# Two pieces of each later modulation vector on TensorE's column tiles, six on VectorE, and the row joined by GpSimd

## The chip, the cores and the metric

The kernel runs on one core of a Trainium2 chip. What counts is the device time of one execution in microseconds (us), as a median of several. Times of single instructions come from one profiled execution, in microseconds from the start of its span unless marked ns. TensorE (PE) has a queue of its own for weight loads (PEld); VectorE is DVE, ScalarE is ACT, GpSimd is POOL, SyncE is SP. A name with a q behind it (SPq, ACTq) is an engine's issuing of DMAs.

## What is computed

Two transformer-like blocks over 1024 tokens of width 1024, everything in float32. The first block is what matters here:

```python
mod = (jax.nn.silu(c) @ ada_w[l] + ada_b[l]).reshape(bsz, 6, dm)
shift_a, scale_a, gate_a = mod[:, 0, None, :], mod[:, 1, None, :], mod[:, 2, None, :]
shift_f, scale_f, gate_f = mod[:, 3, None, :], mod[:, 4, None, :], mod[:, 5, None, :]
h = rms_norm(x, norm1_g[l]) * (1.0 + scale_a) + shift_a
proj = h @ w_in[l]
y_m = mlstm_group(...)      # recurrence over chunks, with gates from proj
y_p = pool_group(...)       # window means of part of proj, then a product
mix = jnp.concatenate([y_m, y_p], axis=-1) @ w_out[l]
x = x + gate_a * mix        # then a mixture of experts over rms_norm(x)
```

The second block (attention and a feed-forward layer) has a modulation of its own, `silu(c_2) @ w_ada_2 + b_ada_2`. So there are twelve modulation vectors of 1024, each the product of one row of 1024 with a 1024x1024 matrix of 4 MB. Two of them (shift_a, scale_a) are needed at once; the other ten are the "later" vectors.

## The kernel before

The program is a row of phases (`mixer`, `moe`, `attention`, `fox_out_mlp`), with a barrier of all engines behind each of the first. The change lies in `mixer`, lines 131 to 1270.

**The projections.** `proj = h @ w_in` is cut into NT = 17 tiles of 128 columns (`tiles`): u0 to u3, the gates g, o0 to o3, p0 to p3, v0 to v3. Product n is tile n times all 1024 tokens, in two halves of 512, each 8 x 3 matmuls (every float32 factor is split into a high and a low float32r part, `split_mm`, lines 1762 to 1768): 48 matmuls. Tile n of w_in is loaded (`weights`), copied to its high part by ScalarE (`high(n)`, line 536) and its low part is taken by VectorE (`low(n)`, line 761, the tile `w_in_low`). VectorE's iteration n ("slot n") ends with `low(n + 2)`; TensorE waits for it (s_lo) ahead of product n + 2. ScalarE evacuates each half product (`evac`) and turns the products of tiles p into silus of u along the way.

**The later vectors.** The matrix of a vector is cut into eight pieces of 128x1024 floats (512 KB): row 8p + k of the matrix is partition p of piece k. Seven pieces (DK = 7) are summed by VectorE (`piece(j)`, line 757): acc = piece * csil[:, k] + acc, where the bias, or zero on the other partitions, is the first addend. acc holds two vectors in turns. The eighth piece is multiplied on TensorE with csil's last column as a one-column stationary operand (line 1132), and the column of ones sums acc over the partitions onto it (line 1135). The two halves of the row go to bank 6, partition 0, and bank 7, partition 32, two column tiles of the array. ScalarE copies the row from PSUM (`mod_row(b)`, lines 577 and 578) and issues its store to `modulation_rows`.

**The order.** `quota` says how many pieces VectorE sums in each slot, `until` its running sum, and `summed_in[b]` the product behind which TensorE sums vector b: now 2, 3, 5, 6, 8, 9, 10, 11, 12, 13. `mod_row(b)` stands in ScalarE's iteration summed_in[b] + 1, ahead of that iteration's evacuations. SyncE loads the pieces in order into three slots of the tile `v_aug` (`spare`), each when VectorE has used the piece three before; the last piece of a vector goes to a fourth slot, from the same queue (`last_piece`, line 300). A slot has other work too: convolutions of u in slots 1 to 4, the gate rows (`gate_rows`, a chain of recurrences over four partitions) in slot 6 behind low(8), window sums of p in slots 11 to 14. ScalarE's iterations 5 and 7 have Exp and Ln for the gate rows.

**Behind the vectors.** SyncE loads w_out's row blocks over acc, the bias tile and x_square (`out_weights`), GpSimd multiplies them with the gate row (`gated_weights`, line 472), then builds the first decay matrix (`decay_log`, line 455), and the loop over eight chunks of tokens starts.

## Time and profile before

| | us |
|---|---|
| median of 3 executions | 2497.85 |
| all three | 2503.66, 2495.33, 2497.85 |
| the profiled execution | 2499.09 |
| its span | 2497.5 |
| TensorE busy | 2400.2 (96%) |
| VectorE busy | 1915.3 (77%) |
| ScalarE busy | 1354.0 (54%) |
| GpSimd busy | 590.3 (24%) |

A row of the profile names line, engine, operation, output and inputs; behind "x" stands how many instructions it merges. In a timeline the first number is the start, the second the time from the first start to the last end; in brackets stands how long the engine was idle ahead of it and what ended this. Matmuls are pipelined, so that 0.39 us of one matmul overlap with the next; how far apart they start tells their pace. A float32 matmul leaves two records.

### The profile page before, as it was taken

What the parts mean: (1) busy time and instruction counts of PE and PEld (TensorE: products, weight loads), DVE (VectorE), ACT (ScalarE), POOL (GpSimd) and SP (SyncE); (2) the same over time, 40 slices, a digit from 0 to 9 for tenths busy, and PEclk for the clock granted to TensorE, in tenths of its full rate; (3) what the DMA queues carried; (4) which work ended last, traced back from release to release, by engine and by line L of the source; (5) the groups of instructions that cost most, each with busy time, mean ns of one, the idle gap of its engine ahead of it and who ended that gap; (6) DMA issues with size and microseconds to landing.
All of it is one profiled execution on the core that took longest, in us unless ns stands there. A gap on an engine that the chain in (4) does not pass through costs nothing. (4 is left out here: it accounts for less than half of the span.)

```text
span 2497.5 us, 33891 instructions
## 1 busy us (share of the span) xinstructions
PE 2400.2 (96%) x11969; PEld 1979.8 (79%) x11969; DVE 1915.3 (77%) x2471; ACT 1354.0 (54%) x1924; POOL 590.3 (24%) x492
## 2 busy tenths in 40 slices
PE   7999999899999999999989999999999999999999
PEld 4766678678888887886688999997788888878887
DVE  4876668678989989897877888887766666657786
ACT  3243323357777777775676676776434444444332
POOL 2000444143333233332711111110042333400000
PEclk8999999999999999999999999999999999999999
DMA  6778255589878899998521111113332443587864
GB/s 253 237 246 297 102 208 206 227 318 397 336 270 308 307 398 395 411 394 337 193 69 51 52 52 51 52 39 116 129 110 86 152 167 139 188 314 260 304 252 152
DMA packets 181316, 535.36 MB, mean 214 GB/s; under 512 B 17711, under 2 KB 77715, under 8 KB 167881
## 3 DMA queue, kind: packets, MB, share of 16 engines
q1 hardware_dynamic: 147260, 462.82, 50.6%
q0 software_dynamic: 12592, 45.63, 4.8%
q10 hardware_dynamic: 21340, 25.29, 2.9%
q8 instruction: 75, 1.23, 0.2%
q14 instruction: 49, 0.39, 0.1%
HBM read 443.38 MB, written 90.33 MB: 214 GB/s over the span
## 5 line engine op out<-in xcount | busy, mean ns | idle before, releaser
L1766 PE MATMUL psum<-w_high,block_hT_high 128*128 128x512 f32 x576 | 232.5, 404 | 6.9 <-DVE w_low L1384 5.7
L1384 DVE TENSOR_TENSOR w_low<-first_w_up,w_high 128x2048 fp32r<-128x2048 f32 x72 | 186.5, 2628 | 53.1 <-ACT w_high L1378 53.1
L1768 PE MATMUL psum<-w_high,block_hT_low 128*128 128x512 f32 x576 | 225.3, 391 | 0.0
L1767 PE MATMUL psum<-w_low,block_hT_high 128*128 128x512 f32 x576 | 224.8, 390 | 0.0
L1766 PE MATMUL psum<-w_qkv_high,fox_hT_high 128*128 128x384 f32 (+1 forms) x512 | 181.6, 355 | 8.5 <-DVE w_qkv_low L2613 3.4
L1384 DVE TENSOR_TENSOR w_low<-first_w_gate,w_high 128x2048 fp32r<-128x2048 f32 x74 | 168.6, 2282 | 19.6 <-ACT w_high L1378 19.4
L1766 PE MATMUL psum<-w_mlp_out_high,hidden_part_high 128*128 128x512 f32 x448 | 174.5, 390 | 3.3 <-DVE hidden L4011 1.8
L1480 POOL TENSOR_TENSOR block_out<-block_out,late_rows 128x1024 f32<-128x1024 f32 x35 | 92.7, 2648 | 359.6 <-ACT block_out L1644 359.6
L1378 ACT ACTIVATE w_high<-first_w_gate 128x2048 fp32r<-128x2048 f32 x74 | 141.2, 1912 | 65.4 <-DMA first_w_gate<-in_w_expert_gate 61.6
L1767 PE MATMUL psum<-w_mlp_out_low,hidden_part_high 128*128 128x512 f32 x448 | 174.3, 389 | 0.0
L1768 PE MATMUL psum<-w_mlp_out_high,hidden_part_low 128*128 128x512 f32 x448 | 174.3, 389 | 0.0
L1768 PE MATMUL psum<-w_qkv_high,fox_hT_low 128*128 128x384 f32 (+1 forms) x512 | 173.7, 339 | 0.0
L1767 PE MATMUL psum<-w_qkv_low,fox_hT_high 128*128 128x384 f32 (+1 forms) x512 | 173.7, 339 | 0.0
L1766 PE MATMUL psum<-mix_hT_high,w_in_high 128*128 128x512 f32 x400 | 163.0, 408 | 3.6 <-DVE w_in_low L761 2.1
L1384 DVE TENSOR_TENSOR w_low<-first_w_down,w_high 128x2048 fp32r<-128x2048 f32 x70 | 156.8, 2277 | 2.4 <-ACT w_high L1378 2.4
L1767 PE MATMUL psum<-mix_hT_low,w_in_high 128*128 128x512 f32 x400 | 157.6, 394 | 0.0
L3763 ACT ACTIVATE hidden_part_high<-hidden_part 128x1024 fp32r<-128x1024 f32 x54 | 57.2, 1060 | 175.8 <-PE psum L1768 171.6
L1766 PEld LDWEIGHTS psum<-w_high,block_hT_high 128*128 128x128 f32 x576 | 108.4, 188 | 42.2 <-DVE w_low L1384 19.2
L1378 ACT ACTIVATE w_high<-first_w_down 128x2048 fp32r<-128x2048 f32 x70 | 130.5, 1915 | 19.5 <-DMA first_w_down<-in_w_expert_down 12.8
L1378 ACT ACTIVATE w_high<-first_w_up 128x2048 fp32r<-128x2048 f32 x72 | 133.9, 1915 | 0.6 <-DMA first_w_up<-in_w_expert_up 0.6
L1768 PEld LDWEIGHTS psum<-w_high,block_hT_low 128*128 128x128 f32 x576 | 108.1, 188 | 23.9
L1767 PEld LDWEIGHTS psum<-w_low,block_hT_high 128*128 128x128 f32 x576 | 108.3, 188 | 20.9 <-issue 0.2
(524 smaller groups left out, 6732.3 us busy)
## 6 DMA issues: line engine op xcount, KB each, us to landing
first_w_gate<-in_w_expert_gate SPq DMA_DIRECT2D x32, 2048.0 KB, 10.0
first_w_up<-in_w_expert_up SPq DMA_DIRECT2D x32, 2048.0 KB, 10.4
first_w_down<-in_w_expert_down SPq DMA_DIRECT2D x31, 2048.0 KB, 10.5
w_mlp_out_quarters<-in_w_mlp_out SPq DMA_DIRECT2D x78, 512.0 KB, 7.0
hidden_part<-hidden_parts SPq DMA_DIRECT2D x54, 512.0 KB, 4.4
v_aug<-in_w_ada SPq DMA_DIRECT2D x48, 512.0 KB, 5.1
expert_rows<-block_out POOLq DMA_DIRECT2D x34, 512.0 KB, 8.3
v_aug<-in_ada_w SPq DMA_DIRECT2D x32, 512.0 KB, 4.8
```

The lines of the kernel that those rows point to most:

```text
L1378: act.activation(wh[:, par, half], raw[kind][:, half], ACT.Copy).then_inc(s_wh, 1)
L1384: dve.tensor_tensor(wl[:, par, half], raw[kind][:, half], wh[:, par, half].bitcast(F32), ALU.subtract).then_inc(s_wl, 1)
L1480: pool.tensor_tensor(ob[:, u, :], ob[:, u, :], grow, ALU.mult).then_inc(s_om, 1)
L1766: pe.matmul(out, sh, mh, start=start, stop=False)
L1767: pe.matmul(out, sh, ml, start=False, stop=False)
L1768: return pe.matmul(out, sl, mh, start=False, stop=stop)
L3763: act.activation(sph[u][:, ij], h_split(gc, ij), ACT.Copy).then_inc(q_sh, 1)
```

## The change

Of a later vector's eight pieces VectorE now sums six (DK = 6). The seventh is loaded into the second half of the bias tile, the eighth into the fourth slot, both by ScalarE's queue (`last_pieces`, called at the start of the `mod_row` of the vector before). TensorE multiplies the seventh onto partitions 64 (bank 6) and 96 (bank 7) and the eighth, with the sums of acc, onto 0 and 32 as before. ScalarE copies both rows, one into acc's own first partition; GpSimd adds them (`join_row`) and issues the store. A vector's first piece on VectorE waits for the join of the vector two before, where it waited for its sums; the biases share one row. The quotas are cut anew: slots 0 to 8 had 7, 4, 3, 4, 3, 7, 6, 6, 6 pieces and have 7, 4, 3, 3, 3, 6, 6, 2, 6. `summed_in` becomes 2, 3, 5, 6, 7, 9, 10, 11, 12, 13. The loads of w_out all wait for the last row's store.

```diff
...
         later = [(0, q) for q in range(2, 6)] + [(1, q) for q in range(6)]
-        DK = KT - 1
+        DK = KT - 2
         NP = DK * len(later)
-        quota = [7, 4, 3, 4, 3, 7] + [6] * (NT - 6)
+        quota = [7, 4, 3, 3, 3, 6, 6, 2] + [6] * (NT - 8)
         until = [min(NP, sum(quota[:n + 1])) for n in range(NT)]
...
 
-        def sums_row(hf):
-            return bank[6 + hf][32 * hf:32 * hf + 1, :]
+        def sums_row(hf, at=0):
+            return bank[6 + hf][at + 32 * hf:at + 32 * hf + 1, :]
 
...
 
-                def last_piece(b):
-                    l, q = later[b]
-                    if b == 0:
-                        sp.wait_ge(s_gain, 1)
-                    else:
-                        sp.wait_ge(s_ms, b)
-                    sp.dma_start(spare[:, 3, :], ada[l][:, DK, q * D:(q + 1) * D]).then_inc(s_ml, 16)
-
                 def piece(j):
...
                     if k == 0:
-                        if b < 2:
+                        if b == 0:
                             sp.wait_ge(s_f0, 1)
                         else:
-                            sp.wait_ge(s_ma, DK * (b - 2) + 1)
-                        sp.dma_start(bt[0:1, b % 2, :], ada_bias[l][:, q * D:(q + 1) * D]).then_inc(s_mb[b % 2], 16)
+                            sp.wait_ge(s_ma, DK * (b - 1) + 1)
+                        sp.dma_start(bt[0:1, 0, :], ada_bias[l][:, q * D:(q + 1) * D]).then_inc(s_mb[0], 16)
                     if j >= 3:
...
                         piece(sent)
-                        if sent % DK == 2 and sent > DK:
-                            last_piece(sent // DK - 1)
                         sent += 1
-                    if n + 1 < NT and until[n + 1] == NP and until[n] < NP:
-                        last_piece(len(later) - 1)
 
...
                 sp.wait_ge(s_ms, len(later))
-                for n in range(4):
+                sp.wait_ge(s_mw, 16 * len(later))
+                for n in range(5):
                     out_weights(n)
-                sp.wait_ge(s_mw, 16 * len(later))
-                out_weights(4)
                 sp.dma_start(shift2, mods[SHIFT_F:SHIFT_F + 1, :].to_broadcast([P, D])).then_inc(d_rows, 16)
...
                     pool.tensor_tensor(stat[:, t, 1:2], stat[:, t, 0:1], mhalf[:], ALU.pow).then_inc(s_rs, 1)
+                def join_row(b):
+                    l, q = later[b]
+                    pool.wait_ge(s_me, b + 1)
+                    pool.tensor_tensor(mrow, mrow, acc[0:1, b % 2, :], ALU.add).then_inc(s_mx, 1)
+                    pool.wait_ge(s_mx, b + 1)
+                    pool.dma_start(mods[6 * l + q:6 * l + q + 1, :], mrow).then_inc(s_mw, 16)
+
+                join_row(0)
+                join_row(1)
                 pool.wait_ge(cv, 4 * HM)
...
                 pool.memset(rr[:, 3, 0:S:P], 0.0).then_inc(r_z, 1)
+                for b in range(2, len(later)):
+                    join_row(b)
 
...
 
+                def last_pieces(b):
+                    l, q = later[b]
+                    if b == 0:
+                        act.wait_ge(s_gain, 1)
+                    act.dma_start(bt[:, 1, :], ada[l][:, DK, q * D:(q + 1) * D]).then_inc(s_ml, 16)
+                    act.dma_start(spare[:, 3, :], ada[l][:, DK + 1, q * D:(q + 1) * D]).then_inc(s_ml, 16)
+
                 def mod_row(b):
-                    l, q = later[b]
                     act.wait_ge(s_ms, b + 1)
+                    if b + 1 < len(later):
+                        last_pieces(b + 1)
                     if b >= 1:
                         act.wait_ge(s_mw, 16 * b)
+                    act.activation(acc[0:1, b % 2, 0:HALF], sums_row(0, 64), ACT.Copy)
+                    act.activation(acc[0:1, b % 2, HALF:D], sums_row(1, 64), ACT.Copy)
                     act.activation(mrow[:, 0:HALF], sums_row(0), ACT.Copy)
                     act.activation(mrow[:, HALF:D], sums_row(1), ACT.Copy).then_inc(s_me, 1)
-                    act.wait_ge(s_me, b + 1)
-                    act.dma_start(mods[6 * l + q:6 * l + q + 1, :], mrow).then_inc(s_mw, 16)
 
...
                 weights(2)
+                last_pieces(0)
                 act.wait_ge(par, 16 * 8)
...
                     if k == 0:
-                        dve.wait_ge(s_mb[b % 2], 16 * (b // 2 + 2))
+                        dve.wait_ge(s_mb[0], 16 * (b + 2))
                         if b >= 2:
-                            dve.wait_ge(s_ms, b - 1)
-                        added = bt[:, b % 2, :]
+                            dve.wait_ge(s_mx, b - 1)
+                        added = bt[:, 0, :]
                     else:
...
                         if summed_in[b] == n:
-                            pe.wait_ge(s_ml, 16 * b + 16)
+                            pe.wait_ge(s_ml, 32 * b + 32)
                             if b >= 1:
...
                             for hf in range(2):
-                                pe.matmul(sums_row(hf), csil[:, l, DK:KT], spare[:, 3, hf * HALF:(hf + 1) * HALF], start=True, stop=False)
+                                pe.matmul(sums_row(hf, 64), csil[:, l, DK:DK + 1], bt[:, 1, hf * HALF:(hf + 1) * HALF], start=True, stop=True)
+                            for hf in range(2):
+                                pe.matmul(sums_row(hf), csil[:, l, DK + 1:KT], spare[:, 3, hf * HALF:(hf + 1) * HALF], start=True, stop=False)
                             pe.wait_ge(s_ma, DK * (b + 1))
```

## Rows read from the trace of the kernel before

**Rows 1.** The page: the chain that ended last, share of the span by engine.

```profile
PE 27%; DVE 1%; DMA 1%; issue 0%; ACT 0%; SPq 0%; DVEq 0%; ACTq 0%
```

**Rows 2.** Busy time of each engine by stage: stretch, length, busy (count), clock, DMA share, GB/s.

```profile
84.50:169.00 84.50, 82.61 (x370) 62.47 (x369) 69.05 (x57) 30.51 (x40) 1.05 (x2) 1.00 0.71 225
169.00:253.40 84.40, 75.74 (x313) 51.22 (x311) 58.03 (x53) 28.72 (x40) 0.00 (x0) 0.94 0.84 281
253.40:297.40 44.00, 41.88 (x179) 31.74 (x178) 24.16 (x26) 10.80 (x16) 19.00 (x9) 1.00 0.28 102
```

**Rows 3.** Timeline of TensorE: start, length, what, idle time ahead and releaser.

```profile
95.36 1.03 PE L1132 MATMUL psum<-v_aug,c_silu 128*1 128x512 f32 x4
96.21 1.03 PE L1135 MATMUL psum<-mod_acc,ones 128*1 128x512 f32 x4
...
175.57 1.87 PE L1132 MATMUL psum<-v_aug,c_silu 128*1 128x512 f32 x4 [2.81 <-DMA v_aug<-in_w_ada]
177.23 1.61 PE L1135 MATMUL psum<-mod_acc,ones 128*1 128x512 f32 x4
180.95 0.50 PE L1766 MATMUL psum<-mix_hT_high,w_in_high 128*128 128x512 f32 x1 [2.11 <-DVE w_in_low L761]
...
193.64 1.03 PE L1132 MATMUL psum<-v_aug,c_silu 128*1 128x512 f32 x4
...
223.06 1.87 PE L1132 MATMUL psum<-v_aug,c_silu 128*1 128x512 f32 x4 [2.66 <-DMA v_aug<-in_w_ada]
...
251.60 1.03 PE L1132 MATMUL psum<-v_aug,c_silu 128*1 128x512 f32 x4
...
264.47 1.88 PE L1069 MATMUL psum<-yT,wpool 128*128 128x512 f32 x4
```

**Rows 4.** Groups by line: busy us, mean ns, idle time before them and its releasers.

```profile
L1132 PE MATMUL psum<-v_aug,c_silu 128*1 128x512 f32 x40 | 12.0, 680 | 7.8 <-DMA v_aug<-in_w_ada 6.5 <-DMA v_aug<-in_ada_w 1.2
```

**Rows 5.** Timeline of VectorE, slots 6 and 7.

```profile
152.28 4.06 DVE L757 SCALAR_TENSOR_TENSOR mod_acc<-v_aug,c_silu,mod_acc 128x1024 f32<-128x1024 f32 x3 [4.23 <-DMA v_aug<-in_w_ada]
156.26 1.22 DVE L761 TENSOR_TENSOR w_in_low<-w_in_tile,w_in_high 128x1024 fp32r<-128x1024 f32 x1
...
169.24 1.28 DVE L757 SCALAR_TENSOR_TENSOR mod_acc<-v_aug,c_silu,mod_acc 128x1024 f32<-128x1024 f32 x1
...
179.67 1.22 DVE L761 TENSOR_TENSOR w_in_low<-w_in_tile,w_in_high 128x1024 fp32r<-128x1024 f32 x1
```

**Rows 6.** Timeline of ScalarE and its queue.

```profile
140.99 0.57 ACT L577 ACTIVATE x_square<-psum 1x512 f32<-1x512 f32 x1
...
180.92 0.57 ACTq L545 DMA_DIRECT2D w_in_tile<-in_w_in  x1
181.54 0.60 ACT L566 ACTIVATE sigmoid_oT<-psum 128x512 f32<-128x512 f32 x1 [6.04 <-DVE w_in_low L761]
...
209.62 1.14 ACT L549 ACTIVATE ucT<-ucT,param_cols 128x1024 f32<-128x1024 f32 x1
```

**Rows 7.** Timeline of GpSimd behind the vectors.

```profile
261.69 4.72 POOL L472 TENSOR_TENSOR mod_acc<-mod_acc,w_in_tile 128x1024 f32<-128x1024 f32 x2 [7.97 <-DMA mod_acc<-in_w_out]
...
273.04 3.45 POOL L472 TENSOR_TENSOR x_square<-x_square,w_in_tile 128x1024 f32<-128x1024 f32 x1
284.98 1.04 POOL L455 TENSOR_TENSOR yT<-gate_rows,packed_cols 128x512 f32<-128x512 f32 x1 [8.49 <-issue]
```

**Rows 8.** DMA issues: count, KB each, median us from issue to landing.

```profile
v_aug<-in_w_ada SPq DMA_DIRECT2D x48, 512.0 KB, 5.1
w_in_tile<-in_w_out SPq DMA_DIRECT2D x1, 512.0 KB, 3.4
```

**Rows 9.** Window sums 3 on VectorE beside GpSimd, and TensorE behind them.

```profile
267.48 3.36 DVE L824 TENSOR_TENSOR yT<-yT 128x1023 f32<-128x1023 f32 x1
...
277.75 1.21 DVE L824 TENSOR_TENSOR yT<-yT 128x1016 f32<-128x1016 f32 x1
...
282.02 1.53 PE L1069 MATMUL psum<-yT,wpool 128*128 128x512 f32 x3 [2.12 <-ACT yT L584]
```

More of the change, by code:

```diff
@@ L195, in mixer @@
         s_mp = [sem(f"m_piece{n}") for n in range(3)]
-        s_ma, s_ms, s_me, s_mw, s_ml = [sem("m_" + n) for n in ("acc", "sums", "row", "stored", "last_piece")]
+        s_ma, s_ms, s_me, s_mw, s_ml, s_mx = [sem("m_" + n) for n in ("acc", "sums", "row", "stored", "last_pieces", "row_joined")]
         s_x = [sem(f"y_x{n}") for n in range(4)]
```

## Prediction

> **What bounds the kernel now.** I read the page first, then busy time by stage, then TensorE in order of time, and only then the engines that TensorE waits for. The page [rows 1] is to show that the chain which ended last lies in later phases. The kernel is a row of phases with a barrier behind each, so what the mixer wins or loses reaches the end one for one unless a later wait of the mixer eats it. The stages [rows 2] show the stretch that the change touches: from 84.50 (product 2 begins; product n is the 48 matmuls of w_in tile n) to 253.42 (product 14 begins). TensorE is idle little in the first half (82.61 busy of 84.50), and for 8.7 us of the second, where its granted clock also falls (0.94 on average: mostly 2.4 GHz, 1.2 GHz for short stretches). Behind 253.40 the DMA share is only 0.28: the modulation vectors are over.
>
> In order of time [rows 3] product 14 begins at 251.60 + 1.82 = 253.42. Twelve products at 48 x 0.2267 = 10.9 us (matmul records come 0.227 us apart) are 131 us, ten groups of sums at 1.8 us (95.36 to 97.17) are 18, three groups of transposes 2.6: 151.5 of 168.9 us. **The whole prize is 17.4 us.** Of it 7.8 is TensorE waiting for a vector's last piece [rows 4], 2.11 is a wait for w_in_low of tile 9, 0.6 another wait, and most of the rest is the low clock behind such waits: the eight sum matmuls at 175.57 take 3.3 us for 1.8, those at 223.06 as long, and product 9, from 180.95 to 193.64, takes 12.7 for 10.9.
>
> Why they are late: one SyncE queue loads seven of eight pieces into three slots and must wait for VectorE to free a slot before it can issue anything behind, the last piece too. VectorE [rows 5] takes 1.35 us a piece (4.06 for three) and 1.2 for a w_in_low, and stands still for the ten steps of the gate rows from 157.4 to 169.24; the pieces left over then push w_in_low 9 to 179.67.
>
> **Part 1: VectorE takes six pieces, TensorE two.** Removed: ten VectorE pieces, 13.4 us, none of it on the path by itself. Added: two M=1 matmuls a vector in column tiles 64 and 96. Now two calls in tiles 0 and 32 start together: four L1132 records take 0.85 us (95.36 to 96.21), where four records of a 128-column fp32 product, L1069, take 1.72 [rows 3]. All four tiles side by side cost nothing; in pairs, 0.85 x 10 = 8.5 us, less where TensorE waits anyway. I take 0 to 1, since the second passes and the next loads start as soon as their own tile is free, and keep 8.5 for the range.
> The Trainium skill (TensorEngine Tiling (Array Packing), Key Properties) says that different tiles load weights and multiply in parallel, and gives 128x32 mode four tiles: by it the term is 0. The trace shows it for two tiles only; no row of before has four.
>
> **Part 2: the last two pieces go to ScalarE's queue.** They no longer stand behind slot waits. The waits of 7.8 us go, and with them the low clock of the 223.06 group (1.5). The price: each DMA issue holds ScalarE for about 0.5 us (ACTq 0.57 at 180.92, next activation at 181.54, [rows 6]). I take 0.9 for two pieces of plain rows, ahead of the copies of the row. With two more copies, mod_row grows from 1.2 to 0.9 + 4 x 0.59 = 3.3 us. Evacuation of a product's first half is due 5.4 us into it, so this hides; what is queued behind it matters below.
>
> **Part 3: GpSimd joins.** No row has its add on 1 partition. Nearest is 128x1024, 4.72 us for two [rows 7]; bounds 1.0 (the 128x512 adds) and 3.4 (the slowest 128x1024 one, beside VectorE); I take 2.4, since ScalarE's copy of 1x512 takes what its 128x512 takes (0.57 and 0.60, [rows 6]): one partition is no cheaper. The store is 0.6 us of issue, and its landing must lie between 1 and 8.3 us (a 512 KB store from that queue). The next mod_row stands 7 us later, so ScalarE does not wait for it in the middle of the range. Two joins stand ahead of GpSimd's memsets for the gate rows, which VectorE needs only at 157.4; the first two vectors are summed behind products 2 and 3, some 45 us earlier.
>
> **Part 4: the new wait.** VectorE may start vector b only when the row of b-2 is joined (s_mx). Before, it waited for the sums alone. Behind this wait stand four pieces and the w_in_low of tile n+2, and behind that TensorE. Let T be the end of product n that carries vector b-2's sums. Sums are done at T+1.9; ScalarE by then has an evacuation, a w_in_high and, in tiles p, a silu (1.14, [rows 6]), and starts mod_row at T+2.65, done T+5.9; the join is done at T+8.4. VectorE does three pieces from full slots (4.0 us). The fourth is asked for when the first is used, T+9.7, and lands 4.8 to 5.1 later ([rows 8]: median 5.1): used by T+15.9, w_in_low at T+17.1. TensorE wants it at T + 1.9 + 10.9 + 1.8 = T+14.6. This circle (sums, row, join, pieces, w_in_low, product) matters: **wherever a vector starts in each slot, TensorE can be held to (10.9 + 17.1)/2 = 14.0 us a slot**, about the pace of before (product 10 at 193.64 + 1.8 + 0.85 = 196.3, product 14 at 253.42: 14.3 for each of four), against 12.8 if TensorE ruled.
>
> **The chain, in profile time.**
> Until product 6 (136.5) I change nothing: the wait in slot 2 is about 3 us and the slack before w_in_low 6 takes it.
> Slot 5: vector 4 starts here now. Its wait, for row 2, meets ScalarE in Exp and Ln with their table loads until 140.99 [rows 6]. 140.99 + 3.3 + 2.4 = 146.7; two pieces and w_in_low 7 end at 150.6. Product 7 began at 150.71, so the 1.2 us of the wait removed at product 6's end comes back as this one.
> Slot 6: six pieces, the last three bound by landing (5 us behind use of the slot): w_in_low 8 at 163.5, before 157.4; product 8 at 163.7, before 161.7.
> Gate rows: 11.9 us to 175.4. Then two pieces where there were six with landing waits (169.24 to 179.67), w_in_low 9 at 179.3: product 9 at **179.3 against 180.95**, behind an idle stretch of near 5 us, so with the low clock again (+1.7, between the 1.5 and 1.8 of before).
> Product 9 ends at 192.0, product 10 starts at 194.7 (196.3 before). Silu needs a table load here (1.28): row 5 is joined at 201.8 and w_in_low 11 is out at 210.5, where TensorE is ready at 207.6. Product 11 at 210.5, with the low clock; product 12 at 225.0; product 13 waits for row 7 (223.2 + 17.1): 240.3; product 14 at 253.2 to 254.9.
> Before: 253.42. So over the stage **0 to +1.5 us, I take +0.5**: 10 to 12 us of waits removed, as much put in.
>
> **Part 5: the tail.** W_out loads now all wait for the last store. Before, the first was in use at 261.69, 8.3 us behind product 14's start [rows 7]. Now they are asked for at product 13's end + 1.9 + 2.4 + 2.4 + 0.6 + 2 to 4, or 8 to 10 us behind product 14's start, and the first lands 5 us later. GpSimd's five gatings (15 us) start near +14 instead of +8.3 and end at +29, still ahead of their successor decay_log (284.98, +31.5), so nothing there. But window_sums 3 starts at +14 and then lies wholly beside them: one add took 3.36 us for 1.21 beside GpSimd [rows 9], and TensorE already waits 2.12 us for that block's end at 282.02. One more such collision is 2.15; none is 0. I take +0.7.
> The Trainium skill (SBUF — State Buffer, section Who interferes with whom) says that a VectorE op with two SBUF inputs and a GpSimd op that reads SBUF exclude each other for a whole instruction. The trace agrees (3.36 against 1.21). By the page each of ten joins may cost the sum such a wait. What the rows give is one wait of 2.15 us a meeting, and in the slots that decide VectorE stands idle for the join, so there is nothing to meet.
>
> **Sum:** +0.5 + 0.7 = +1.2 on an execution of 2499.09 us (span 2497.5 and 1.6 around it), which was 1.2 above the median. From the median 2497.85 that is **2499 us**.
>
> **Rivals.**
> 1. *The circle is shorter, faster.* If the join takes 1.0 us, issues cost ScalarE little and the fourth piece lands in 3.4 (the one w_out load that is alone on its queue, [rows 8]), the circle shrinks by 1.4 + 0.7 + 1.5 = 3.6: T+13.5, under TensorE's T+14.6. Then product 9 starts at 177.5 and product 14 at 177.5 + 1.7 + 13.65 + 4 x 12.8 = 244 to 246: 7.5 to 9.5 less, **2489 to 2491**. Against it: one partition was no cheaper on ScalarE, and the DMA is busy 0.84 of 169 to 253. 0.27 for the case, 0.22 that it passes 0.3%.
> 2. *Landing under load, slower.* ScalarE's 1 MB and a w_in tile are asked for just as VectorE's fourth piece is. A piece at 152.28 was waited for 4.23 us [rows 5]; my circle has 2.1. If 4.2 is the rule, w_in_low 8, 11 and 13 come 2.1 us later each and the delays add up, since 11 hangs on product 9 and 13 on 11: 1.2 + 6.3 + 1.7 for one more low clock = +9.2, **2507**, 2506 to 2508. It decides from a wait of about 4 us on. 0.17.
> 3. *The four tiles run in pairs.* +0.85 where TensorE rules (some six vectors): +5, **2503**, still within. 0.12.
> The forecast's case has 0.44. Faster by over 0.3% (7.5 us, about what a measurement can tell) 0.22, slower 0.19 (rival 2's 0.17 and 0.02 for pairs with late landings), the same 0.59. The range of 8 in 10 goes from 2488 (rival 1 nearly whole) to 2508.
>
> **What would show it.** Right: L1132 no longer waits for DMA; VectorE's idle time shows the join at the first piece of vectors 4, 6, 7 and 8; TensorE waits for w_in_low before products 9, 11 and 13; product 14 begins between 252 and 256. Part 1: eight records of the new and old first sums within 0.9 us, or 1.7. Part 3: the join 2.4 us. Wrong if w_in_low comes in time throughout: then product 14 begins before 247; or if product 9 begins behind 182.

## The result: slower, by 0.46%

| | before | after |
|---|---|---|
| median, us | 2497.66 (12 executions) | 2509.43 (12 executions) |
| lowest to highest | 2492.85 to 2504.61 | 2502.80 to 2516.67 |
| profiled execution / its span | 2499.09 / 2497.5 | 2508.58 / 2507.0 |

The ratio is 1.0046, 95% interval 1.0033 to 1.0059. The forecast was 2499, or +1.2 us and no change to be measured, with a range up to 2508. The measured +11.8 us has the small sign that was forecast, but it is ten times the size, clear of the noise and above the range.

I cut the mixer into three parts. "Stage" runs from the first sums (the end of product 2) to the start of product 14; "tail" from there to the first matmul of the loop over chunks; the rest is the span behind that.

| | first sums at | product 14 at | stage | loop at | tail | rest |
|---|---|---|---|---|---|---|
| before | 95.36 | 253.42 | 158.06 | 299.83 | 46.41 | 2197.7 |
| after | 93.15 | 257.75 | 164.60 | 309.87 | 52.12 | 2197.1 |

Stage **+6.5** (forecast +0.5), tail **+5.7** (forecast +0.7), start-up -2.2, rest -0.5: together the 9.5 us between the spans. The first sums come anywhere between 91.9 and 95.7 in the profiles of this study, so the start-up's part is no effect of the change.

The chain that ended last, by engine, on the page of after (answers [rows 1]):

```profile
PE 28%; DVE 1%; issue 0%; ACT 0%; DVEq 0%
```

As in [rows 1], it says only that the end of the program is TensorE's. The stages of after (stretch, length, busy and count of PE, PEld, DVE, ACT, POOL, then clock, DMA share, GB/s; answer [rows 2]):

```profile
84.50:169.00 84.50, 80.85 (x380) 59.54 (x379) 62.12 (x50) 34.13 (x47) 13.72 (x10) 1.00 0.75 243
169.00:253.40 84.40, 72.02 (x311) 52.43 (x310) 53.03 (x47) 33.32 (x48) 14.55 (x9) 0.94 0.77 254
253.40:297.40 44.00, 39.05 (x160) 27.97 (x159) 31.67 (x29) 11.37 (x17) 22.75 (x12) 0.92 0.28 106
```

TensorE is idle 12.4 us in the second stretch where it was 8.7, at the same mean clock (0.94). VectorE does less in the first two (115.2 us against 127.1), and TensorE still waits for it. The waits of the two engines between 84 and 260, groups by line (answer [rows 4]; busy us, mean ns, idle time ahead and its releasers):

```profile
L1775 PE MATMUL psum<-mix_hT_high,w_in_high 128*128 128x512 f32 x193 | 78.5, 407 | 13.9 <-DVE w_in_low L768 13.9
L1139 PE MATMUL psum<-mod_bias,c_silu 128*1 128x512 f32 x40 | 10.3, 590 | 1.4 <-DMA v_aug<-in_w_ada 1.4
...
L764 DVE SCALAR_TENSOR_TENSOR mod_acc<-v_aug,c_silu,mod_acc 128x1024 f32<-128x1024 f32 x45 | 59.7, 1326 | 20.2 <-DMA v_aug<-in_w_ada 14.8 <-DMA v_aug<-in_ada_w 3.2
L764 DVE SCALAR_TENSOR_TENSOR mod_acc<-v_aug,c_silu,mod_bias 128x1024 f32<-128x1024 f32 x8 | 10.3, 1285 | 32.9 <-POOL x_square L435 32.4 <-DMA v_aug<-in_w_ada 0.5
```

The wait of [rows 4] went from 7.8 to 1.4, as forecast. In its place TensorE waits 13.9 us for w_in_low, and VectorE stands 32.4 us for GpSimd's join at the first pieces of vectors (before: 35.8 us for pieces in flight, none for a row).

Here is one slot in full, from w_in_low 10 to w_in_low 11 (start, length, what; idle time ahead and its releaser). VectorE and GpSimd:

```profile
193.91 1.22 DVE L768 TENSOR_TENSOR w_in_low<-w_in_tile,w_in_high 128x1024 fp32r<-128x1024 f32 x1
...
202.28 2.38 POOL L435 TENSOR_TENSOR x_square<-x_square,mod_acc 1x1024 f32<-1x1024 f32 x1 [16.22 <-ACT x_square L586]
...
204.79 1.28 DVE L764 SCALAR_TENSOR_TENSOR mod_acc<-v_aug,c_silu,mod_bias 128x1024 f32<-128x1024 f32 x1 [6.24 <-POOL x_square L435]
206.18 2.67 DVE L764 SCALAR_TENSOR_TENSOR mod_acc<-v_aug,c_silu,mod_acc 128x1024 f32<-128x1024 f32 x2
209.84 1.28 DVE L764 SCALAR_TENSOR_TENSOR mod_acc<-v_aug,c_silu,mod_acc 128x1024 f32<-128x1024 f32 x1 [0.98 <-DMA v_aug<-in_w_ada]
211.04 1.22 DVE L768 TENSOR_TENSOR w_in_low<-w_in_tile,w_in_high 128x1024 fp32r<-128x1024 f32 x1
```

and ScalarE with its queue in the same slot:

```profile
195.16 0.55 ACTq L543 DMA_DIRECT2D w_in_tile<-in_w_in  x1
195.75 0.60 ACT L562 ACTIVATE yT<-psum 128x512 f32<-128x512 f32 x1 [8.93 <-DVE w_in_low L768]
195.86 0.55 ACTq L574 DMA_DIRECT2D mod_bias<-in_w_ada  x1
196.25 1.05 ACT L534 ACTIVATE w_in_high<-w_in_tile 128x1024 fp32r<-128x1024 f32 x1
196.45 0.92 ACTq L575 DMA_DIRECT2D v_aug<-in_w_ada  x1
197.31 1.28 ACT L547 ACT_TABLE_LOAD   x1
198.61 1.15 ACT L547 ACTIVATE ucT<-ucT,param_cols 128x1024 f32<-128x1024 f32 x1
199.79 0.59 ACT L583 ACTIVATE mod_acc<-psum 1x512 f32<-1x512 f32 x1
...
201.60 0.59 ACT L586 ACTIVATE x_square<-psum 1x512 f32<-1x512 f32 x1
...
212.29 0.55 ACTq L543 DMA_DIRECT2D w_in_tile<-in_w_in  x1
```

Read it as a ring. ScalarE stands 8.93 us behind VectorE's w_in_low 10, because it issues the load of the w_in tile three ahead (L543), whose buffer w_in_low frees. Only then come its evacuation, w_in_high, a silu with its table load, and the four copies of the row; then the join; then VectorE's four pieces and w_in_low 11, which ends at 212.26, and ScalarE issues the next such load at 212.29. **The ring holds no product of TensorE.** It takes 17.1 us here, 16.5 and 16.0 in the next two slots, where sums and a product need 12.8. Within these three rings VectorE also waits for pieces in flight, for 0.98, 1.88 and 1.10 us; the rest is work and hand-overs. TensorE's starts of products 9, 10, 11, 13 and 14 follow it (answers [rows 3]; product 12 starts at 228.80):

```profile
178.83 0.67 PE L1775 MATMUL psum<-mix_hT_high,w_in_high 128*128 128x512 f32 x1 [4.39 <-DVE w_in_low L768]
...
195.18 0.50 PE L1775 MATMUL psum<-mix_hT_high,w_in_high 128*128 128x512 f32 x1 [0.71 <-DVE w_in_low L768]
...
212.31 0.50 PE L1775 MATMUL psum<-mix_hT_high,w_in_high 128*128 128x512 f32 x1 [3.51 <-DVE w_in_low L768]
...
244.81 0.50 PE L1775 MATMUL psum<-mix_hT_high,w_in_high 128*128 128x512 f32 x1 [1.39 <-DVE w_in_low L768]
...
257.75 0.50 PE L1775 MATMUL psum<-mix_hT_high,w_in_high 128*128 128x512 f32 x1
```

In the tail (answers [rows 7, 9]; VectorE's last w_in_low and its window sums 3 beside GpSimd's gatings, TensorE behind them):

```profile
269.19 5.70 POOL L470 TENSOR_TENSOR mod_acc<-mod_acc,w_in_tile 128x1024 f32<-128x1024 f32 x2 [4.59 <-DMA mod_acc<-in_w_out]
...
270.58 2.05 DVE L768 TENSOR_TENSOR w_in_low<-w_in_tile,w_in_high 128x1024 fp32r<-128x1024 f32 x1 [4.36 <-ACT w_in_high L534]
...
272.62 3.34 DVE L831 TENSOR_TENSOR yT<-yT 128x1023 f32<-128x1023 f32 x1
276.00 2.22 DVE L830 COPY yT<-yT 128x2 f32<-128x2 f32 x1
...
282.78 2.23 DVE L830 COPY yT<-yT 128x8 f32<-128x8 f32 x1
...
289.18 3.75 PE L1076 MATMUL psum<-yT,wpool 128*128 128x512 f32 x4 [4.95 <-ACT yT L590]
292.72 1.92 PE L1065 MATMUL psum<-ident,yT 128*128 128x128 f32 x8
```

and in the kernel before the same w_in_low, and the last small copy, free of GpSimd:

```profile
266.25 1.25 DVE L761 TENSOR_TENSOR w_in_low<-w_in_tile,w_in_high 128x1024 fp32r<-128x1024 f32 x1 [5.03 <-ACT w_in_high L536]
...
277.68 0.17 DVE L823 COPY yT<-yT 128x8 f32<-128x8 f32 x1
```

The w_in_low begins 12.83 us behind product 14's start in both kernels. In after it takes 2.05 us where it took 1.25, and the block meets GpSimd four times (3.34, 2.22, 2.25, 2.23) where it met it three times (3.36, 2.23, 2.25). That makes 2.8 us: TensorE resumes at 31.43 behind product 14's start, 28.60 before. It waited 4.95 us where it waited 2.12, and now the clock is low behind it: 3.54 us from the first of these four matmuls to the next group, which took 1.79 before, 1.57 for the next eight (0.79), and 0.35 more for the half product. That is the other 2.9 us of the tail's 5.7. I read these by starts, since records overlap: at full clock a matmul's record lasts 0.39 us and the next starts 0.23 behind it. The granted clock from 289.1 to 294.3 is 0.50 (1.2 GHz); before it was 1.00 from 282.0 to 284.6.

The length of the wait alone does not decide this clock. From these four matmuls to the half product behind them the kernel before takes 2.58 us, at full clock, behind its wait of 2.12; y3 and z2 take as long behind waits of 2.83 and 2.84. But x3 takes 1.7 us more behind a wait of 2.11, y4 1.7 behind 2.07 and x2 1.6 behind 4.99. What decides it was not found, so this half of the tail's loss is measured but not explained.

### The profile page after: what moved, and what is told of

Its sections match the earlier page's. It is cut to its first block and busy times, and to the rows that moved or that the text cites. A ratio compares the mean times of both kernels' runs of the same rounds, so it can differ in the third digit from the quotient of the medians.

```text
span 2507.0 us, 33974 instructions
## 1 busy us (share of the span) xinstructions
PE 2399.9 (96%) x12009; PEld 1980.9 (79%) x12009; DVE 1910.2 (76%) x2461; ACT 1367.6 (55%) x1944; POOL 626.5 (25%) x512
## 5 line engine op out<-in xcount | busy, mean ns | idle before, releaser
L1775 PE MATMUL psum<-mix_hT_high,w_in_high 128*128 128x512 f32 x400 | 164.4, 411 | 14.8 <-DVE w_in_low L768 13.9
```

Of the source, the lines that this page charges most:

```text
L1775: pe.matmul(out, sh, mh, start=start, stop=False)
```

## The experiments

Theory R (ring): the wait for the join closes a ring through ScalarE's wait for w_in_low, the row, the join and the pieces; what lengthens the ring lengthens each slot, and without the wait the slots go back to TensorE's 12.8 us. Rivals: late loads (the fourth piece), the four column tiles, ScalarE's issues, VectorE's load around the gate rows.

All stages and tails, in us, with medians and ratios to the kernel before (95% interval):

| | stage | tail | median | ratio |
|---|---|---|---|---|
| before | 158.1 | 46.4 | 2497.7 to 2498.9 | |
| after | 164.6 | 52.1 | 2509.43 | 1.0046 [1.0033, 1.0059] |
| x1_weights_later | 163.3 | 52.0 | 2510.30 | 1.0052 [1.0036, 1.0068] |
| x2_own_row | 153.0 | 50.9 | 2498.74 | 1.0005 [0.9986, 1.0024] |
| x3_own_row_tail | 154.5 | 48.1 | 2490.08 | 0.9977 [0.9963, 0.9991] |
| x4_no_join | 151.1 | 44.4 | 2486.49 | 0.9955 [0.9942, 0.9969] |
| y1_queue_only | 153.0 | 51.2 | 2496.04 | 0.9990 [0.9976, 1.0005] |
| y2_join_twice | 172.9 | 49.8 | 2520.10 | 1.0082 [1.0063, 1.0100] |
| y3_old_quotas | 162.3 | 47.0 | 2504.82 | 1.0026 [1.0010, 1.0043] |
| y4_pieces_by_gpsimd | 149.6 | 48.1 | 2489.12 | 0.9961 [0.9948, 0.9974] |
| z1_tail_after_join | 166.0 | 49.6 | 2506.02 | 1.0029 [1.0013, 1.0046] |
| z3_no_join_gpsimd | 151.1 | 44.4 | 2487.34 | 0.9951 [0.9934, 0.9969] |
| z2_old_quotas_gpsimd | 158.9 | 47.1 | 2498.37 | 0.9998 [0.9983, 1.0013] |

Stage and tail are of one execution each; a median is of 6 to 12 executions (12 to 29 for the kernel before, measured anew beside each group of runs, so that ratios compare better than medians). The two need not add up: the rest of the span varies between 2189.3 and 2204.3 from profile to profile. Kernels with the same code up to product 14 differ in the stage by 1.4 us (after, z1) and 1.5 (x2, x3), so a difference of that size shows nothing.

**x1_weights_later.** The load that ScalarE waits for moves behind its row.

```diff
                         if summed_in[b] + 1 == n:
                             mod_row(b)
+                    if n >= 3 and n + 2 < NT:
+                        weights(n + 2)
...
                     evac(n, 0)
-                    if n + 3 < NT:
-                        weights(n + 3)
```

> The changed kernel, but ScalarE issues the load of w_in tile n+2 behind the row of its iteration n instead of tile n+3 between its two evacuations. In the changed kernel's trace mod_row stands behind an issue that waits for w_in_low (195.13 low done, 195.16 issue, 195.75 evacuation, 199.79 row, 204.7 join, 212.26 next low: one closed round of 16 to 17 us a slot). Theory 'closed round through ScalarE': the row comes right behind the sums, product 10 to product 14 takes about 14 us a slot instead of 16.2, so 6 to 8 us less over the stage and 2502 to 2504 in all (the tail's loss stays). Rival 'landing of the pieces under load': nothing changes, 2509. Rival 'GpSimd and VectorE collide': nothing changes either, 2509.

A miss: 2510.3. The later slots did open (product 11 to product 14 took 41.2 us, 45.4 in after), but tiles now came late, ScalarE waited 5.13 and 4.17 us for them, and TensorE waited more for w_in_low 11 than ever:

```profile
190.39 1.06 ACT L534 ACTIVATE w_in_high<-w_in_tile 128x1024 fp32r<-128x1024 f32 x1 [5.13 <-DMA w_in_tile<-in_w_in]
...
215.71 0.80 PE L1775 MATMUL psum<-mix_hT_high,w_in_high 128*128 128x512 f32 x1 [7.44 <-DVE w_in_low L768]
```

One wait was swapped for another, so this run decides nothing between the theories. The next two change the ring itself.

**x2_own_row.** The seventh piece's row is copied to a buffer of its own, not into acc, so VectorE waits for the sums alone again; join, column tiles and queues stay.

```diff
-        mrow = sq[0:1, :]
+        mrow, seventh = sq[96:97, :], zrow[96:97, 1, :]
...
-                    pool.tensor_tensor(mrow, mrow, acc[0:1, b % 2, :], ALU.add).then_inc(s_mx, 1)
+                    pool.tensor_tensor(mrow, mrow, seventh[:], ALU.add).then_inc(s_mx, 1)
...
-                    act.activation(acc[0:1, b % 2, 0:HALF], sums_row(0, 64), ACT.Copy)
+                    act.activation(seventh[:, 0:HALF], sums_row(0, 64), ACT.Copy)
...
-                            dve.wait_ge(s_mx, b - 1)
+                            dve.wait_ge(s_ms, b - 1)
```

> The changed kernel, but the seventh piece's row is copied beside acc (to another place in SBUF), so VectorE's next vector waits for the sums alone and no longer for the join. Closed round: the waits of 4 to 8.6 us for the join at the first piece of vectors 4 to 9 go, the stage to product 14 gets 6 to 9 us shorter, the tail stays: 2500 to 2503. Rival 'landing under load': the pieces then wait for DMA instead, at most 2 us less, 2507 to 2509. Rival 'collision': joins now run beside a busy VectorE, ten meetings of up to 2.15 us: 2509 or slower.

It took 2498.74, a little better than expected. VectorE's wait for the join is gone and TensorE's for w_in_low fell from 13.9 to 4.4:

```profile
L764 DVE SCALAR_TENSOR_TENSOR mod_acc<-v_aug,c_silu,mod_bias 128x1024 f32<-128x1024 f32 x8 | 12.4, 1550 | 3.1 <-DMA v_aug<-in_w_ada 2.9
L764 DVE SCALAR_TENSOR_TENSOR mod_acc<-v_aug,c_silu,mod_acc 128x1024 f32<-128x1024 f32 x45 | 60.1, 1337 | 34.8 <-DMA v_aug<-in_w_ada 29.5 <-DMA v_aug<-in_ada_w 3.9
...
L1775 PE MATMUL psum<-mix_hT_high,w_in_high 128*128 128x512 f32 x209 | 82.6, 395 | 4.4 <-DVE w_in_low L768 4.4
```

The stage is 11.6 us shorter than in after and 5.0 shorter than before. So the new wait cost more than the whole loss of the stage, and hid a gain of 5.0.

Theory R had the slots go back to 12.8 us, and that is not so. From product 9 to 13 they take 14.2 to 16.8 us, 60.4 in all (66.0 in after, 59.5 before). Over the stage VectorE now waits 36.3 us for pieces in flight, where it waited 18.5 in after and 35.8 before: with the ring open, late loads stand in its place. By the trace they hold these slots; no run tests that apart. The gain over the kernel before lies ahead, from product 6 to 9: 38.6 us against 44.4.

**y2_join_twice.** After, with one more GpSimd operation of the join's size (times one) ahead of each join.

```diff
+                    pool.tensor_tensor(acc[0:1, b % 2, :], acc[0:1, b % 2, :], ones[0:1, 0:1].to_broadcast([1, D]), ALU.mult).then_inc(s_my, 1)
+                    pool.wait_ge(s_my, b + 1)
                     pool.tensor_tensor(mrow, mrow, acc[0:1, b % 2, :], ALU.add).then_inc(s_mx, 1)
```

> The changed kernel with a second GpSimd instruction of the join's size (a multiplication of the row by one, 2.4 us and some 0.3 of semaphore) ahead of each join: it doubles the suspected cost. 'VectorE's wait for the join closes a round': each round that is closed gets 2.7 us longer: slots 5, 8, 9, 10 and 11, so 10 to 14 us more, 2519 to 2523, and x2_own_row's gain is this. 'The join itself is off the path': less than 2 us, 2509 to 2511.

It took 2520.1. GpSimd's two operations and TensorE's products 10 and 11:

```profile
199.33 0.50 PE L1778 MATMUL psum<-mix_hT_high,w_in_high 128*128 128x512 f32 x1 [1.70 <-DVE w_in_low L771]
...
206.42 1.88 POOL L436 TENSOR_TENSOR mod_acc<-mod_acc,ones 1x1024 f32<-1x1024 f32 x1 [13.75 <-ACT x_square L589]
208.38 2.37 POOL L438 TENSOR_TENSOR x_square<-x_square,mod_acc 1x1024 f32<-1x1024 f32 x1
...
218.30 0.80 PE L1778 MATMUL psum<-mix_hT_high,w_in_high 128*128 128x512 f32 x1 [4.83 <-DVE w_in_low L771]
```

The added operation is 1.88 us, and product 10 to product 11 grew from 17.13 to 18.97: by 1.84, one for one. The next two slots grew by 1.03 and 1.75, the one from 6 to 7 by 1.94 and the one from 7 to 8 by 1.33; from 8 to 10 none did. The stage is 8.3 us longer than in after, less than the 10 to 14 expected; the median is 10.7 longer. x2 and this run show the ring from both sides: opened, it lets the stage go; lengthened, the slots that wait for the join grow by 1.0 to 1.9 us, all but the one from 9 to 10.

**x3_own_row_tail.** x2, and four of w_out's loads wait for the last sums only, as before the change.

> As x2_own_row, and the first four loads of w_out wait for the last sums alone, as in the kernel before. From product 14 to the loop's first product the changed kernel takes 52.1 us where before takes 46.4. If that 5.7 us is the later loads that push all five gatings on GpSimd over VectorE's window sums, this kernel gives 4 to 6 us back against x2_own_row: 2495 to 2498. If the tail's loss has another cause (the pace of the last slots), it is within 1 us of x2_own_row.

The edit is the one shown for z1 below, without its wait for the join, on x2. It took 2490.08, faster than expected. The tail fell from 50.9 to 48.1 and TensorE's wait there from 4.99 to 2.11. The medians differ by 8.7 us. The tail has 2.8 of it and the stage, with the same code, is 1.5 longer in this profile. The rest I can't place: between the two profiled executions it lies in start-up (3.8) and later phases (11.2), which this edit doesn't touch. So the evidence for this edit is the tail, and not the whole step between the medians.

**z1_tail_after_join.** The tail's edit alone on after: the four loads wait for the last join, not for its store to land.

```diff
-                sp.wait_ge(s_mw, 16 * len(later))
-                for n in range(5):
+                sp.wait_ge(s_mx, len(later))
+                for n in range(4):
                     out_weights(n)
+                sp.wait_ge(s_mw, 16 * len(later))
+                out_weights(4)
```

> The changed kernel, with one edit: the first four loads of w_out wait for the last join (which reads their target) instead of the landing of the last row's store. In the changed kernel the last join ends at 263.6 and GpSimd's gating starts at 269.19. Theory A (the tail's 5.7 us come from the w_out loads that start too late, so that gating lies beside window sums 3): the loads start about 2.5 us earlier, gating starts at 266 to 267, one of the four collisions (2.2 us each) goes, the tail is 49.5 to 51 us instead of 52.1: 2506 to 2508 us. Theory B (the tail is set by the later sums and joins themselves, the store's landing is hidden): tail 52, 2509 to 2510 us.

It took 2506.02 with a tail of 49.6: as theory A says. The intervals of z1 and after overlap, so it is the tail that tells them apart. Gating starts 9.8 us behind product 14 (11.4 in after), VectorE's block meets it three times instead of four, TensorE resumes at 30.08 (31.43), waits 3.60 where it waited 4.95, and the low clock behind takes 1.7 us where it took 2.9. To let the loads go at the last sums was not tried on after: they land in acc, where the seventh row waits for the join.

**x4_no_join.** x3 without GpSimd: both pieces are added in turn into the same row of PSUM as the sums of acc, and ScalarE copies one row and stores it. TensorE pays for it, in column tiles 0 and 32 alone.

```diff
-                                pe.matmul(sums_row(hf, 64), csil[:, l, DK:DK + 1], bt[:, 1, hf * HALF:(hf + 1) * HALF], start=True, stop=True)
+                                pe.matmul(sums_row(hf), csil[:, l, DK:DK + 1], bt[:, 1, hf * HALF:(hf + 1) * HALF], start=True, stop=False)
...
-                                pe.matmul(sums_row(hf), csil[:, l, DK + 1:KT], spare[:, 3, hf * HALF:(hf + 1) * HALF], start=True, stop=False)
+                                pe.matmul(sums_row(hf), csil[:, l, DK + 1:KT], spare[:, 3, hf * HALF:(hf + 1) * HALF], start=False, stop=False)
```

> TensorE takes the same two pieces, but one behind the other into the same PSUM row with the sums of acc: no join, no store from GpSimd, two copies in mod_row as before, the tail's loads as before. One product pair in series is 0.86 us a vector, 8.6 us for ten if TensorE rules everywhere. If the closed round and the tail are the whole loss, this gains them and pays the 8.6 in part: 2494 to 2500. If the six-to-two split itself or the cut of the quotas costs, it stays above 2503.

It took **2486.49, faster than both kernels** and than expected. Its first two stretches (the same columns as above):

```profile
84.50:169.00 84.50, 84.50 (x379) 60.10 (x378) 67.97 (x57) 31.28 (x42) 1.05 (x2) 1.00 0.73 243
169.00:253.40 84.40, 84.40 (x374) 59.85 (x373) 54.12 (x53) 29.34 (x42) 2.36 (x2) 1.00 0.85 288
```

TensorE has work in every microsecond of the first two stretches, and the granted clock is full. The second passes cost their 0.86 us a vector, 8.6 in all. Side by side in four tiles they cost nothing, but leave two rows to be joined. The tail is 2.0 us shorter than before, 3.7 shorter than with joins (x3): TensorE resumes behind window sums 3 at 26.60 and not at 28.59, waits 0.2 and not 2.11 us, and has no low clock behind it (1.7 us in x3). Gating starts 6.0 us behind product 14 here and 7.0 in x3; the 2.0 us by which TensorE resumes later there are those of the last w_in_low, which takes 3.35 us beside a gating, 1.36 here.

**z3_no_join_gpsimd.** x4 with the last two pieces issued from GpSimd's queue.

> The kernel without a join (both TensorE pieces added in turn into the one row, x4), with the last two pieces issued from GpSimd's queue, which has little to do there, instead of ScalarE's. In x4 TensorE has no wait between 94 and 256. Theory A (x4 is at TensorE's own pace there, nothing is left to win in these stages): product 14 begins within 1 us of x4's 245.2, 2485 to 2488 us. Theory B (ScalarE's 1 us of issue a vector still delays the tail or the row's stores): 1 to 3 us faster than x4, 2483 to 2485.

It took 2487.34, product 14 at 244.93: theory A. Nothing is left to win from issues once TensorE has no wait.

**y4_pieces_by_gpsimd.** x3 (with join and four tiles) with that same move.

> x3_own_row_tail, but the two last pieces are issued from GpSimd's queue as soon as the sums before them are done, not from ScalarE's, where they stand behind the wait for w_in_low. In x3's trace TensorE waited 1.71, 1.12 and 2.05 us for them. If the place in ScalarE's order is the cause: these waits go and 2 to 5 us with them, 2485 to 2488. If the DMA engines are the bound there (share 0.84 over the last slots of before), the waits stay or move to VectorE's pieces: 2489 to 2491. Against it: GpSimd writes its descriptors itself and may hold VectorE up.

It took 2489.12 with the shortest stage of all, 149.6, and no wait for the last pieces; TensorE waits only 4.3 us for w_in_low. The time lies in the second range of its expectation, but the trace shows the first cause: the waits for last pieces went, and VectorE waits less for its own (28.4 us, 36.1 in x3). By the stage it is 1.5 us ahead of x4, no more than the scatter; its tail of 48.1 against 44.4 gives that back, with the last join in it. The intervals of the two times overlap.

**y1_queue_only.** Before, with its one last piece issued by ScalarE at the start of the `mod_row` of the vector before; nothing else of the change.

```diff
-                        if sent % DK == 2 and sent > DK:
-                            last_piece(sent // DK - 1)
...
                     act.wait_ge(s_ms, b + 1)
+                    if b + 1 < len(later):
+                        last_piece(b + 1)
```

> The kernel before with one part of the change alone: the last piece of each vector is issued from ScalarE's queue, in mod_row of the vector before. VectorE still sums seven, no join, old quotas, old tail. TensorE waited 7.8 us for last pieces in the kernel before and paid about 3 us of low clock behind these waits. If the place in the queue was their cause: 4 to 8 us faster, 2490 to 2494. If the pieces on VectorE set the pace of the last slots anyway (it waited 37 us for its own pieces between 60 and 310), w_in_low or the sums come late in their place, and it stays within 2 us of before.

It took 2496.04: no change that can be told. The 7.8 us of [rows 4] are gone and the stage is 5.0 shorter, w_in_low 9 coming late (5.20 us) at the place where it did before. But the tail is 4.8 longer: at window sums 3 TensorE waits 4.46 us where it waited 2.12, with the low clock behind (2.5 us by the starts). The trace shows where that comes from:

```profile
259.21 5.70 POOL L460 TENSOR_TENSOR mod_acc<-mod_acc,w_in_tile 128x1024 f32<-128x1024 f32 x2 [10.76 <-DMA mod_acc<-in_w_out]
```

SyncE's loads of w_out stand behind its load of the gate row, which waits for w_in_low 15. That ends 5.1 us behind product 14's start, where it ended 2.5 behind it before, since VectorE's work up to there came forward by less than TensorE's. So gating starts 10.9 us behind product 14 (8.3 before) and meets VectorE's last copy too (2.24 us for 0.17). Two things follow. Moving the last piece gives the stage the same 5.0 us as the whole of x2, so x2's gain in the stage can't be credited to the six-to-two split. And it is no gain in all, because the tail takes it back; what the move is worth with w_out's loads freed earlier, no run shows.

**y3_old_quotas and z2_old_quotas_gpsimd.** x4 and z3 with the quotas of before, 7, 4, 3, 4, 3, 7, 6, ... With six pieces a vector this makes vectors summed behind products 2, 3, 4, 6, 7, 8, 9, ..., so that one more row falls into ScalarE's iterations up to 8.

> x4_no_join with the quotas of the kernel before (7, 4, 3, 4, 3, 7, then 6 a slot until the 60 pieces are done). x4's trace has no wait of TensorE from 94 to 256. If the recut (2 pieces in the slot behind the gate rows, where 6 stood) carries part of x4's gain, w_in_low of tile 9 comes late again and this is 3 to 6 us slower than x4: 2489 to 2492. If the six-to-two split alone is enough, it is within 1 us of x4, 2486 to 2488.

> As z3, with the quotas 7, 4, 3, 4, 3, 7, 6... (those of the kernel before). With ScalarE's queue this order took 2504.82 us, with a 9.37 us wait of TensorE at 184.6 for the last two pieces of vector 5. Theory A (that wait comes from where they are issued: behind ScalarE's gate work, which waits for VectorE's gate rows): issued from GpSimd right behind the sums they are there, the wait at 184.6 goes, 2486 to 2490 us, so that the recut quotas are not needed by VectorE at all. Theory B (VectorE's load around the gate rows needs the recut quotas): w_in_low 9 or the sums of vector 5 come late instead, TensorE waits 5 us or more there, 2494 to 2502 us.

y3 took 2504.82, 18 us more than x4: a clear miss. ScalarE in y3, and TensorE behind it:

```profile
171.70 1.06 ACT L646 ACTIVATE gate_rows<-yT 4x1024 f32<-4x1024 f32 x1 [7.36 <-DVE a_prev L801]
...
176.59 0.45 ACTq L565 DMA_DIRECT2D v_aug<-in_w_ada  x1
...
184.62 1.87 PE L1130 MATMUL psum<-mod_bias,c_silu 128*1 128x512 f32 x4 [9.37 <-DMA v_aug<-in_w_ada]
```

The last pieces of vector 5 hang on the `mod_row` of vector 4, which stands behind the gate rows' Exp, which waits for VectorE until 171.70. In z2 they are issued elsewhere. The 9.37 us are gone, 6.4 us of the 18 come back (in the stages 3.4 of 11.2), and what stays is in part again a row that stands behind that Exp: the sums of the next vector wait for ScalarE's copy out of PSUM, and the low clock follows (1.70 us for each of the groups at 178.42 and 180.12, 0.86 in z3).

```profile
177.39 1.25 PE L1137 MATMUL psum<-mod_bias,c_silu 128*1 128x512 f32 x4 [1.98 <-ACT x_square L583]
...
182.76 0.50 PE L1773 MATMUL psum<-mix_hT_high,w_in_high 128*128 128x512 f32 x1 [0.94 <-DVE w_in_low L766]
```

z2's 2498.37 lies in the range of its theory B, but B's mechanism, a wait of 5 us or more at this place, is not there: beside these 1.98 us TensorE has three waits of 0.9 to 1.7 us for w_in_low. So both theories have a part. By y3's wait of 9.37 us, what the recut quotas buy is above all an order in which no vector is summed behind product 8, where ScalarE is tied to the gate rows. I had priced them by VectorE's load alone.

## Why the prediction was wrong, by its steps

**What bounds the kernel: right.** The prize of the stage was put at 17.4 us before any added work; x4, with 8.6 us of second passes added, is 7.0 below before, so 15.6 of it was there to be had; y4 is 8.5 below.

**Part 1, the tiles: right.** Eight records of the new and the old first sums (start, time to the last end):

```profile
93.15 0.60 PE L1139 MATMUL psum<-mod_bias,c_silu 128*1 128x512 f32 x2
93.16 0.60 PE L1141 MATMUL psum<-v_aug,c_silu 128*1 128x512 f32 x2
93.58 0.60 PE L1139 MATMUL psum<-mod_bias,c_silu 128*1 128x512 f32 x2
93.59 0.60 PE L1141 MATMUL psum<-v_aug,c_silu 128*1 128x512 f32 x2
94.02 1.03 PE L1144 MATMUL psum<-mod_acc,ones 128*1 128x512 f32 x4
```

From 93.15 to 94.02 is 0.87 us, for half as many it was 0.85 [rows 3]. The Trainium skill's rule (TensorEngine Tiling (Array Packing), Key Properties), that different tiles work in parallel, holds here for four.

**Part 2, the queue: right in what goes, too dear in what it costs.** The waits fell from 7.8 to 1.4. I charged ScalarE 0.9 us for two issues; in the slot shown they lie at 195.86 and 196.45, beside its evacuation and w_in_high, and cost next to nothing. Where nothing ran beside them, at 179.35 and 179.74, they held the copies of the row for 1.0 us.

**Part 3, the join: right.** 2.38 us against 2.4; 2.70 to 3.24 for four joins that meet VectorE.

**Part 4, the new wait: the step that failed.** Products 7, 8 and 9 began at 147.74, 163.26 and 178.83 (forecast 150.6, 163.7, 179.3). Counted from the first sums, which came 2.2 us early, product 9 is 1.7 late: in slot 6 VectorE waited for pieces 6.7 us in all, 3.85 of it for one piece, and the slot took 15.5 us for my 13.1. That is rival 2's mechanism, in a small size.
The larger error is behind it. My circle was "sums, row, join, pieces, w_in_low, product", with `mod_row` beginning at T+2.65. The sentence "ScalarE by then has an evacuation, a w_in_high and, in tiles p, a silu" puts these beside the sums. They can't be there: ScalarE's load of the tile three ahead stands ahead of them and waits for the slot's w_in_low, which waits, through the pieces, for the join before. In slot 10 I had the row joined at 201.8, 9.8 us behind product 9's end; it was at 204.66, 13.1 behind it, though the four pieces and w_in_low went faster than I allowed (7.6 us from join to end against 8.7). Product 9 to 10 took 16.4 us (forecast 15.4), 10 to 13 took 49.6 (45.6), 13 to 14 took 12.9 (13.6). So the 6.0 us over the forecast are 1.7 + 1.0 + 4.0 - 0.7. The rows had what was needed: the order of ScalarE's iteration, and its 6.04 us of idle time behind w_in_low in [rows 6]. I read that row for the cost of an issue and not for its wait.

**Part 5, the tail: the mechanism right, the size wrong.** I took 0.7 us out of "none is 0, one more collision is 2.15". One more collision it was, with 0.8 more in the last w_in_low: 2.8 us at TensorE. Gating even started earlier than I had it, 11.4 us behind product 14 and not 14. The low clock behind the wait, another 2.9, was put at nothing in my sum, though I had charged the same thing in the stage. z1 prices the wait for the store's landing at 2.6 us of tail, about half of it low clock; x3, against x2, prices landing and join together at 2.8, none of it low clock.

**The rivals.** Rival 2 gave nearly the right time, 2507, mostly for the wrong reason: in the slots behind product 9 its fourth piece was waited for 0.98, 1.59 and 1.10 us, not 4.2, and VectorE waited for DMA less than before in all (18.5 against 35.8). Rival 1, a shorter circle, had the join at 1.0 us, and it took 2.38; what shortened the circle was another wiring, x2. Rival 3 fell with Part 1.

## What to carry to other kernels

Before you price a new wait, follow the ring that it may close through every engine's program order: from the waiting instruction to what is queued behind it, who waits for that, and what stands on that engine ahead of the instruction that releases you. If the ring comes back to its start without the engine that should set the pace, its length is the pace, and each microsecond in it counts once a slot. And an edit that pays 0.86 us a vector on the bounding engine (x4) can do as well as one that is free there but needs two more engines to finish the work, or better: x4 has 195.5 us of stage and tail, y4 197.7 and x3 202.6. Last, a gain in one stretch counts only if what follows starts earlier too. In y1 it did not, since the next loads hung on another engine's work.

## What I had not expected

- Two DMA issues on ScalarE's queue (0.55 and 0.92 us) overlapped with its activations at 195.75 and 196.25. One behind a wait (195.16) held the next activation until 195.75.
- An operation of GpSimd on one partition, 1x1024, takes 2.38 us, as much as one of the two on 128x1024 in [rows 7] (4.72); with a broadcast second factor it took 1.88.
- Beside a gating, VectorE's copies of 128x2, 128x4 and 128x8 took 2.22 to 2.25 us, with 0.17 for such a copy undisturbed, and so did a 128x4 copy beside the last join (2.24). The Trainium skill (SBUF — State Buffer, section Who interferes with whom) says that copies too can enter a mode which takes the ports shared with GpSimd, and for these the trace agrees. A copy of 128x1 at 272.56 took 0.14, but the gating beside it took 3.36 us for 2.37, so it may itself have been waiting then; whether one column meets GpSimd is not shown. My forecast had looked at the adds alone.
- The kernel's later phases, which none of these edits touch, took between 2189.3 and 2204.3 us from profile to profile, more than most of the effects. The stage and tail of one profile tell a cause better than one time does, down to the 1.5 us by which they scatter.
